# Expert blocks of 64 rows, two experts side by side in the column halves of TensorE

## The reference

```python
TOP_K, D_EXPERT, N_EXPERTS = 2, 512, 32
order = jnp.argsort(expert)                  # the 1024 (token, expert) slots, by expert
sizes = jnp.bincount(expert, length=N_EXPERTS)
buf = zeros.at[dest].set(xt[tok])            # rows of an expert, in blocks
def expert_block(args):                      # one block of rows, one expert
    xb, e = args
    return (jax.nn.silu(xb @ w1[e]) * (xb @ w3[e])) @ w2[e]
ys = ys * gate[order]                        # and added back into its token
```

## Time and profile before

| what | before |
|---|---|
| median of 3 runs | 3597.13 us (3596.42 to 3600.28) |
| profiled execution, its own time | 3597.67 us |
| its span | 3595.8 us |
| PE busy | 3244.9 us, 90% |
| DVE busy | 1885.5 us, 52% |
| ACT busy | 1312.1 us, 36% |
| DMA | 486.33 MB, mean 135 GB/s |
| mean granted TensorE clock | 0.935 |
| expert weights loaded | 96 DMAs of 2048 KB (16 pairs) |

### The profile page before, as it was taken

One profiled execution on the slowest core, in us unless ns is written; L12 is line 12 of the kernel. 1 busy time (PEld: TensorE's weight loads), 2 busy tenths in 40 slices (PEclk: granted clock), 3 DMA queues, 4 the chain that ended last, 5 costly groups with the idle time before them and its releaser, 6 DMA issues.

```text
span 3595.8 us, 35715 instructions
## 1 busy us (share of the span) xinstructions
PE 3244.9 (90%) x14016; PEld 2391.4 (67%) x14016; DVE 1885.5 (52%) x2774; ACT 1312.1 (36%) x1949; POOL 44.4 (1%) x76
## 2 busy tenths in 40 slices
PE   7997899699999967899899899999799988879998
PEld 3645887567767645688665678877477756558776
DVE  5345753556656544423473335554598966443343
ACT  2215223355555533225244222223322255432333
POOL 0000000000000000000000000000000000000000
PEclk9998999699999988799899999999899989789999
DMA  8330001699999951212013125551022211032210
GB/s 298 132 127 1 1 1 49 260 375 385 390 375 386 389 218 62 71 71 94 24 48 116 67 71 187 187 182 63 26 100 70 94 47 36 12 117 94 94 70 24
DMA packets 146804, 486.33 MB, mean 135 GB/s; under 512 B 8176, under 2 KB 11888, under 8 KB 134128
## 3 DMA queue, kind: packets, MB, share of 16 engines
q1 hardware_dynamic: 130544, 438.58, 32.8%
q10 hardware_dynamic: 10368, 24.92, 1.8%
q0 software_dynamic: 5760, 20.97, 1.5%
HBM read 459.28 MB, written 25.17 MB: 135 GB/s over the span
## 4 chain that ended last, share of the span: by engine, by line
PE 83%; DVE 7%; ACT 4%; issue 3%; DMA 1%; SPq 0%; POOL 0%; ACTq 0%; POOLq 0%; DVEq 0%; PEldq 0%
PE bank L456 18%; PE bank L458 17%; PE bank L457 17%; PE bank L1700 5%; PE bank L355 5%; PE bank L2319 3%; PE bank L556 2%; PE bank L1179 2%; PE bank L2972 1%; PE bank L1668 1%; PE bank L2113 1%; PE bank L2112 1%; DMA ring<-in_w_ada 1%; PE bank L550 1%; PE bank L3010 1%
## 5 line engine op out<-in xcount | busy, mean ns | idle before, releaser
L457 PE MATMUL bank<-h_parts,A_parts 128*128 128x512 f32 x1424 | 560.3, 393 | 0.0
L456 PE MATMUL bank<-h_parts,A_parts 128*128 128x512 f32 x816 | 324.5, 398 | 35.8 <-DVE h_parts L3266 13.4
L445 ACT ACTIVATE A_parts<-ring 128x1024 fp32r<-128x1024 f32 x178 | 187.3, 1053 | 463.8 <-PE bank L458 463.0
L458 PE MATMUL bank<-h_parts,ring_parts 128*128 128x512 f32 x896 | 353.9, 395 | 0.0
L452 DVE TENSOR_TENSOR ring_parts<-ring,A_parts 128x1024 fp32r<-128x1024 f32 x178 | 217.5, 1223 | 252.8 <-ACT A_parts L445 252.8
L457 PEld LDWEIGHTS bank<-h_parts,A_parts 128*128 128x128 f32 x1424 | 271.8, 191 | 59.5 <-issue 4.3
L456 PE MATMUL bank<-A_parts 128*128 128x512 f32 x672 | 267.5, 398 | 8.6 <-DVE A_parts L2668 5.2
L1739 DVE TENSOR_TENSOR ring_parts<-ring,h_parts 128x1024 fp32r<-128x1024 f32 x192 | 225.7, 1220 | 42.3 <-ACT h_parts L1802 41.4
L458 PE MATMUL bank<-A_parts,ring_parts 128*128 128x512 f32 x624 | 245.5, 393 | 0.0
L458 PE MATMUL bank<-h_parts,A_parts 128*128 128x512 f32 x576 | 226.6, 393 | 0.0
L457 PE MATMUL bank<-ring_parts 128*128 128x512 f32 x544 | 214.4, 394 | 0.0
(11 more groups left out here) (522 smaller groups left out, 5765.9 us busy)
## 6 DMA issues: line engine op xcount, KB each, us to landing
ring<-in_expert_w SPq DMA_DIRECT2D x64, 2048.0 KB, 9.6
ring<-in_w_in SPq DMA_DIRECT2D x37, 2048.0 KB, 8.0
A<-in_expert_w SPq DMA_DIRECT2D x32, 2048.0 KB, 8.2
ring<-in_w_ada SPq DMA_DIRECT2D x24, 2048.0 KB, 12.5
ring<-in_w_ff SPq DMA_DIRECT2D x16, 2048.0 KB, 8.5
slot_rows<-A ACTq DMA_DIRECT2D x32, 512.0 KB, 9.6
ring<-in_w_ffn_gate SPq DMA_DIRECT2D x5, 2048.0 KB, 7.9
ring<-in_w_ffn_up SPq DMA_DIRECT2D x5, 2048.0 KB, 8.9
```

The costliest lines, as they stand in the source:

```text
L445: act.activation(parts(s.shaped(high(s.q % 2))), s.raw(), ACT.Copy).then_inc(sem("split_high"), 1)
L456: pe.matmul(out, parts(w_high), parts(r_low), start=start, stop=False)
L457: pe.matmul(out, parts(w_high), parts(r_high), start=False, stop=False)
L458: return pe.matmul(out, parts(w_low), parts(r_high), start=False, stop=stop)
```

## The change

A block now holds 64 rows (`CAP`), so there is room for 15 spill blocks, `N_BLK` = 48 and `N_PAIR` = 24. A pair of blocks is one tile of 128 rows: the even block in rows 0 to 63, the odd one in rows 64 to 127. It is gathered by one DMA, turned once, and written back by one DMA. Each weight product of a block has 64 stationary columns; the even block's goes to output partitions 0 to 63 (column half 0 of the array), the odd one's to 64 to 127, and the products of the two blocks alternate in program order. All of them are whole fp32 matmuls; the splits on ScalarE and VectorE are gone. The list of token numbers is built per pair in the same two halves.

```diff
+CAP = 64
+N_SPILL = (2 * T - N_EXP) // CAP
 N_BLK = N_EXP + N_SPILL + 1
+N_PAIR = N_BLK // 2
...
-            for i in range(2 * TT):
-                mm = pe.matmul(bank[5][:, 0:N_BLK], on_rem(i), on_blk(i), start=(i == 0), stop=(i == 2 * TT - 1))
+            for s in range(2):
+                for i in range(2 * TT):
+                    mm = pe.matmul(bank[5][CAP * s:CAP * (s + 1), 0:N_PAIR], on_rem(i), on_blk(i)[:, s:N_BLK:2],
+                                   start=(i == 0), stop=(i == 2 * TT - 1))
...
-            for j in range(2, TT):
-                step(dve.scalar_tensor_tensor(n_spill, cnt, float(P * j), n_spill, ALU.is_gt, ALU.add))
+            for j in range(2, T // CAP):
+                step(dve.scalar_tensor_tensor(n_spill, cnt, float(CAP * j), n_spill, ALU.is_gt, ALU.add))
...
-                for s, j in ((0, 0), (0, 1), (1, 0), (1, 1), (0, 2), (1, 2)):
-
-                    sp.wait_ge(sem(f"moe_{('gated', 'upped', 'downed')[j]}"), 2 * i + s + 1)
-                    load(j, s, mats[j][bass.ds(es[s], 1), :, :].rearrange("e p n -> (e p) n"))
+                for j in range(3):
+                    sp.wait_ge(sem(f"moe_{('gated', 'upped', 'downed')[j]}"), i)
+                    for s in range(2):
+                        load(j, s, mats[j][bass.ds(es[s], 1), :, :].rearrange("e p n -> (e p) n"))
...
+            def into(i, j):
+
                 if j == 0:
...
+                    pe.wait_ge(sem("moe_rows_t"), i + 2)
+                    pe.wait_ge(sem("moe_hid"), i + 1)
+                for s in range(2):
+                    pe.wait_ge(sem(f"moe_w{j}{s}"), 16 * i + 16)
+                for k in range(KD):
+                    for s in range(2):
+                        mm = pe.matmul(bank[4 + j][HALF[s], :], rows_t[:, k * P + CAP * s:k * P + CAP * (s + 1)],
+                                       moe_w(s, j)[:, k * T:(k + 1) * T], start=(k == 0), stop=(k == KD - 1))
+                mm.then_inc(sem(("moe_gated", "moe_upped")[j]), 1)
...
+            def down(i):
+
+                pe.wait_ge(sem("moe_hid"), i + 1)
                 for f in range(4):
...
+                    mm = pe.transpose(head(bank[6][:], f), hid[:, f:D_EXP:4], sq("ident"))
                 mm.then_inc(sem("moe_hid_turned"), 1)
...
+                for h_ in range(2):
+                    for f in range(4):
+                        for s in range(2):
+                            mm = pe.matmul(bank[h_][HALF[s], :], hid_t[:, f * P + CAP * s:f * P + CAP * (s + 1)],
+                                           wt[s][:, f, h_ * T:(h_ + 1) * T], start=(f == 0), stop=(f == 3))
+                mm.then_inc(sem("moe_downed"), 1)
+
+            rows_turn(0)
+            into(0, 0)
+            into(0, 1)
             with pe.Fori(1, n) as i:
...
+                rows_turn(i)
+                down(i)
+                into(i, 0)
+                into(i, 1)
+            down(n)
```

More of the change, by code:

```diff
@@ L1624, in moe_sync @@
             sp.wait_ge(*seen("zero_rows", 1))
-            for b in range(N_EXP, N_BLK):
+            for b in range(N_EXP * CAP // P, N_BLK * CAP // P):
                 sp.dma_start(slot_rows[b * P:(b + 1) * P, :], A[:, 28:30, :].rearrange("p a n -> p (a n)"))\
@@ L1672, in gated @@
-            def gated(i, m, pieces=range(4)):
-                s, j = MOE_IN[m]
-                if j == 0:
[L1676 to L1683, removed]
@@ L1725, in moe_pe @@
-            down(n, 0, 0)
-            hid_turn(n, 1, 2)
-            down(n, 0, 1)
-            down(n, 1, 0)
-            down(n, 1, 1)
+                wt = [moe_w(s, 2).rearrange("p (f n) -> p f n", f=4) for s in range(2)]
+                for h_ in range(2):
+                    for f in range(4):
+                        for s in range(2):
+                            mm = pe.matmul(bank[h_][HALF[s], :], hid_t[:, f * P + CAP * s:f * P + CAP * (s + 1)],
+                                           wt[s][:, f, h_ * T:(h_ + 1) * T], start=(f == 0), stop=(f == 3))
@@ L1778, in moe_dve, with gate, hid_copy @@
-            gate(n, 1, 2)
-            hid_copy(n, 1, 2)
+            def gate(i):
+                dve.wait_ge(sem("moe_silu"), i + 1)
+                dve.wait_ge(sem("moe_upped"), i + 1)
+                dve.tensor_tensor(hid, gate_act, bank[5][:], ALU.mult).then_inc(sem("moe_hid"), 1)
+            def hid_copy(i):
+                dve.wait_ge(sem("moe_hid_turned"), i)
+                dve.tensor_copy(hid_t, bank[6][:]).then_inc(sem("moe_hid_t"), 1)
+            rows_copy(0)
+            gate(0)
@@ L1781, in moe_act @@
+            with dve.Fori(1, n) as i:
+                hid_copy(i)
+                rows_copy(i)
+                gate(i)
+            hid_copy(n)
         def moe_act(act):
             n = pairs(act)
-            act.sem_inc(sem("moe_y_read"), 4)
-            act.sem_inc(sem("moe_silu"), 2)
-            for s in range(2):
-                act.sem_inc(sem(f"moe_out{s}"), 16)
-            act.wait_ge(sem("spill_zeroed"), 16 * (N_BLK - N_EXP))
-            out_v = slot_rows.rearrange("(b p) n -> b p n", p=P)
@@ L1848, in moe_act, with silu @@
-            for s in range(2):
-                y_copy(n, s)
-                y_out(n, s)
-            for s in range(2):
-                act.wait_ge(sem(f"moe_out{s}"), 16 * n + 16)
+            act.sem_inc(sem("moe_y_read"), 1)
+            act.sem_inc(sem("moe_out"), 16)
+            act.wait_ge(sem("spill_zeroed"), 16 * (N_BLK - N_EXP) * CAP // P)
+            out_v = slot_rows.rearrange("(b p) n -> b p n", p=P)
+            def silu(i):
+                act.wait_ge(sem("moe_gated"), i + 1)
+                act.wait_ge(sem("moe_hid"), i + 1)
+                act.activation(gate_act, bank[4][:], ACT.Silu).then_inc(sem("moe_silu"), 1)
@@ L1853, in moe_act @@
+            silu(0)
+            with act.Fori(1, n) as i:
+                out(i)
+                silu(i)
+            out(n)
+            act.wait_ge(sem("moe_out"), 16 * n + 16)
             act.sem_inc(sem("moe_written"), 1)
```

212 lines of the change are left out of this document (52 added, 160 removed).

## The result

The changed kernel takes 3539.09 us (median of 4 runs, 3538.3 to 3542.87) against 3596.78 (3596.24 to 3600.28) beside it: a ratio of 0.9841, interval 0.9825 to 0.9856, 57.7 us or 1.6% faster. The forecast was 3561.6 us, in a range from 3538 to 3600: the time lies in the range, but only 1 us from its fast end. The profiled execution, the slowest of the four, took 3542.87 us with a span of 3541.0, 54.8 us under the profiled one of before.

What follows compares the result with a forecast made beforehand. The prediction took TensorE to bound the kernel before, the DMA after: 698.2 + 17 x 33.0 + 14.6 put the loop's end at 1273.8 us against 1309.87, 36 us earlier, so 3561.6 us, range 3538 to 3600.

Steps and rivals of the forecast that it cites:

- TensorE gives up the bound to the DMA: Expert loop: TensorE bound at 38.32 us a pair before; afterwards its 24 us falls below the DMA's 33.0.
- Two halves at a time: Expert products: the two column halves run together, factor 2, lower bound 1.6, so 48 products take 20.6 us.
- 24 us of TensorE per pair: Expert loop, TensorE: 20.6 us of products, 1.3 of transposes and 2 of standing still per pair.
- 18 pairs, and what two of them cost: Expert loop: four spill blocks of 64 rows make 18 pairs in place of 16, costing 66 us.
- No buffer comes late: Expert loop's weight loads: buffers come free in time, so fewer waits and SP's in-order queue cost nothing.
- The round of 33.0 us: Expert loop, DMA per pair: 32.5 us of transfers plus 0.5; bounds 31.7 below, 34.6 or 35.1 above.
- four small transfers: Gathers and results of a pair before: 7.2 us of DMA share, 1.8 each; two stay, 3.6 us.
- the loop's turn: Expert loop: 0.5 us per round added to the 32.5 us of DMA transfers.
- Ahead of the loop: Before the expert loop: comparisons add net 1.3 us, first w1 product at 689.1 against 690.06 before.
- Behind it: From the last w2's arrival to the loop's end: landing, last down products, copies, DMA and next load, 14.6 us.
- Rival 1: Expert loop: DMA gives no more than 388 GB/s, round 35.1 us, no change at 3597 us; chance 0.08.
- Rival 3: Expert loop: idling TensorE stays at 1.2 GHz, some 3774 us; 0.12 shared with non-overlapping halves and slower DMA.

Runs made afterwards that it cites:

- e9: Changed kernel with both blocks' products in column half 0, the odd block's in another PSUM bank: 3766.62 us, one run.
- e4: Changed kernel with w2 not loaded again, every pair using the first pair's w2 matrices: 3419.55 us, ratio 0.9506.
- e3: Changed kernel with each pair's 0.524 MB result written a second time to an unused tensor: 3561.94 us, ratio 0.9905.
- e8: Changed kernel with two of the next block's first four loads started once w1's buffers are free, two after the final gathers: 3535.83 us.

## Why the prediction was right, and what was mis-sized

- **TensorE gives up the bound to the DMA: right.** 428 GB/s at a share of 1.01 in place of 381 at 0.96.
- **Two halves at a time: right.** Records 0.04 us apart, and pairs of them 0.43; e9 gives the price of the contrary. The small 64- and 32-column products of the earlier trace rows had been a true witness for 512 columns. I had kept 1.6 as a bound; it was 2.
- **24 us of TensorE per pair: right**, 23.5 in e4.
- **18 pairs, and what two of them cost: right.** 66 forecast, 63.7 by two rounds and 60.7 measured by leaving them out.
- **No buffer comes late: right.** SP's loads follow one another through the loop, and TensorE waits for landings alone.
- **The round of 33.0 us: too long by 1.12.** This is the step that failed, by the size of one term. It took 7.2 us of share for four small transfers, 1.8 each, and called this "slower than their bytes". That came from subtracting the weights at their fastest, 29.6 us, from a share of 0.96, 36.8 us, as if the whole share were work. The rest lay elsewhere: a result has 1.28 to 1.29 us of share in all three kernels, while the weights had 31.8 in the kernel before and have 29.5 now. So the 29.6 was right for full engines, and 1.8 was not the price of a small transfer; e3 says the same, 1.15 to 1.27. The sum with what the queues now show: (29.5 + 1.28 + 1.29) / 1.008 = 31.8 us, in place of the 32.5 forecast; the measured round of 31.88 leaves next to nothing of the 0.5 for the loop's turn. The price was in the bounds of the prediction, as what the small queues' own share says (1.36 and 1.29), and the result is that bound (31.7 us a round, 3539 us), not the forecast's value. That the range held is thanks to it. 17 x 1.12 = 19.0 us, of the 20.0 by which the loop ended earlier than the forecast's 1273.8.
- **Ahead of the loop: 1.7 us too late.** First product at 687.04, not 689.1. 0.9 of these 2.1 us lie ahead of the change and are chance: the last products before the routing (L1460, L1458 before) start at 651.59 in place of 652.50, and in e8, the same code up to there, at 655.48. From there to the placement it is 21.7 us in place of 20.4, which is the 1.3 forecast for the comparisons. From the placement to the first rows it is 10.4 us in place of 11.4, which had been taken as equal. From the first product to the first reload 9.4 us, forecast 9.1; the clock was partly up already (0.86 from 690 to 695, where the earlier trace rows has 0.53).
- **Behind it: 14.6 forecast, 15.1 measured** from the last bytes of w2 (near 1238.7, where the DMA share falls from 0.88 to 0.08 within 2 us) to 1253.76.
- **Rival 1, 388 GB/s: wrong.** The 388 of the earlier trace rows was no ceiling for the expert weights. The w_in loads behind the loop, with gathers beside them, came near it again (columns as in the stretches above):
```profile
1263.00:1268.00 5.00, 0.00 (x0) 0.00 (x0) 2.20 (x3) 0.00 (x0) 0.65 (x1) 0.50 1.03 403
```
The Trainium skill's limit of 358 GB/s ("DMA: Bandwidth & Descriptors", Specifications) would have made a round an estimated 13.63 / 0.358 = 38.1 us. It is worked out there as half of what two cores share; this kernel runs on one core, and moved 428 GB/s over 480 us.
- **Rival 3, the low clock: half true and free.** The clock falls in the waits, as the Trainium skill says of bursts ("TensorE: Matmul & The Clock Gate", HAM oscillation), and comes back within the batch: 0.91 over the loop. What it takes is taken from a wait that is there anyway.

Where the 56.1 us at the loop's end come from. Before, first product to end is 1309.87 - 690.06 = 619.8 us: 16 rounds of TensorE (613.1) and 6.7 more. After, it is 1253.76 - 687.04 = 566.7: 17 rounds of loads (542.0), since the first pair's weights are there ahead of the loop, and 24.8 for the way to the first reload and from the last landing. 613.1 - 542.0 = 71.1 gained, 18.1 given back at the two ends, 3.0 gained ahead (0.9 of them by chance, as above).

## What to carry to other kernels

When a kernel goes from one bound to the next, the new round is to be summed from bytes at the rate of the cleanest stretch, not from the busy share of a queue that wasn't full: here the weights had 31.8 us of share a pair when the engines were not full and 29.5 when they were, and the difference was not the price of the small transfers. Products for the two column halves of the array with 64 rows each overlapped fully here, so whole fp32 products on blocks of 64 rows cost half as much, as long as what the smaller blocks add (here two pairs, 61 to 64 us) is counted. Once a loop is bound by DMA, look at what else is moved at its ends: loads that wait until the small, urgent transfers are through gave 6 us for one line.

## What the runs showed of the hardware that I had not expected

- Products for the two halves overlap also where they don't alternate in the program: with all eight products (16 records) of one block ahead of the other's the round was 32.18 us, bound by TensorE, against 43.80 with everything in one half and the 23.5 that TensorE needs by itself with the halves alternating (e4). Products even started out of program order, those for a free half ahead of those for a busy one.
- A queue's busy share is not its work: 82.9% and 79.7% for the same 167 MB in the same time, the smaller one with more moved beside it. Per MB of weights it was 2.53, 2.43 and, in the changed kernel, 2.35 us.
- A small write beside a queue of large loads costs the total about its bytes (1.15 to 1.27 us for 0.524 MB, 1.22 by the bytes), but the landing of one went from 2.88 us, with nothing beside it, to 6.43. Where somebody waits for it, the second number counts.
- Rates differ from stage to stage, with the engines at 1.01 or more in each: 428 GB/s over 480 us with the expert weights, 388 for the program's first loads and 403 for w_in beside the gathers. Why is not shown.
